# Two output tiles of a weight slab: alternating the single products between their two PSUM banks

## The reference

```python
# first block (cut)
z = rms_norm(x, g_mix) @ w_in
x = x + concat([mla(z...), hgrn2(z...)]) @ w_o
h = rms_norm(x, g_ffn)
x = x + (silu(h @ w_gate) * (h @ w_up)) @ w_down
x = x + sigmoid(rms_norm(x, g_ple) @ w_ple_gate) * (p @ w_ple_proj)
# second block (cut)
q, k, v, g, u, sv, a_ret, a_sgu = split(_rmsnorm(x, g_pre_mix) @ w_in)
merged = sigmoid(a_ret) * retention(q, k, v, g) @ w_ret_o \
       + sigmoid(a_sgu) * spatial_gating(u, sv) @ w_sgu_o
x = x + _rmsnorm(merged @ w_out, g_post_mix)
x = x + _rmsnorm(conv_gated_mlp(_rmsnorm(x, g_pre_ffn)), g_post_ffn)
```

## Time and profile before

| what | value |
|---|---|
| median of three runs | 1727.41 us |
| time of the profiled execution | 1728.11 us |
| its span, first to last instruction | 1726.8 us |
| mean granted clock of TensorE | 0.979 of full speed |
| TensorE matmul busy | 1646.0 us, 95% of the span, 7857 instructions |
| TensorE weight loads busy | 1355.8 us, 7857 instructions |
| VectorE busy | 882.4 us, 51% |
| ScalarE busy | 653.7 us, 38% |
| shares of the chain that ended last | TensorE 91%, VectorE 5%, ScalarE 2% |

### The profile page before, as it was taken

The page is one execution under the profiler, slowest core; times in us unless marked ns, Lnnn a source line. Parts: engine busy times, 40 slices in busy tenths (PEclk is TensorE's granted clock), DMA queues, the critical chain, the costliest instruction groups (busy, mean ns, idle before and its releaser), DMA issues.

```text
span 1726.8 us, 18642 instructions
## 1 busy us (share of the span) xinstructions
PE 1646.0 (95%) x7857; PEld 1355.8 (79%) x7857; DVE 882.4 (51%) x1168; ACT 653.7 (38%) x796; POOL 11.7 (1%) x25
## 2 busy tenths in 40 slices
PE   7999999999999999998999799999997899999997
PEld 6777677778888888776887698888875688888886
DVE  6556556564444422367526533354343777676323
ACT  4546667342222211254423233223232444444211
POOL 1000000000000000000000000000000000000000
PEclk9999999999999999998999999999998899999998
DMA  4321011123333232322321032212222132222221
GB/s 157 92 74 49 25 49 50 49 98 98 98 98 96 97 97 94 112 74 73 104 74 50 25 104 93 95 57 98 98 98 74 49 98 98 98 95 91 97 96 73
DMA packets 120274, 144.28 MB, mean 84 GB/s; under 512 B 6009, under 2 KB 109776, under 8 KB 120192
## 3 DMA queue, kind: packets, MB, share of 16 engines
q1 hardware_dynamic: 118768, 139.87, 24.7%
q0 software_dynamic: 1232, 3.16, 0.6%
q10 hardware_dynamic: 192, 0.07, 0.0%
HBM read 140.99 MB, written 2.10 MB: 83 GB/s over the span
## 4 chain that ended last, share of the span: by engine, by line
PE 91%; DVE 5%; ACT 2%; issue 1%; DMA 1%; SPq 0%; DVEq 0%; ACTq 0%
PE bank L364 27%; PE bank L366 27%; PE bank L365 27%; PE bank L826 1%; PE bank L585 1%; PE bank L584 1%; PE bank L603 1%; PE bank L651 1%; DVE slab_lo L948 1%; PE bank L809 1%; PE bank L632 1%; PE bank L874 1%; PE bank L402 1%; PE bank L646 0%; DVE tmp L961 0%
## 5 line engine op out<-in xcount | busy, mean ns | idle before, releaser
L364 PE MATMUL bank<-h_hi,slab_hi 128*128 128x512 f32 x1320 | 527.3, 399 | 20.5 <-DVE h_lo L953 10.4
L366 PE MATMUL bank<-h_hi,slab_lo 128*128 128x512 f32 x1320 | 519.3, 393 | 0.0
L365 PE MATMUL bank<-h_lo,slab_hi 128*128 128x512 f32 x1320 | 519.3, 393 | 0.0
L948 DVE TENSOR_TENSOR slab_lo<-slab_raw,slab_hi 128x2048 fp32r<-128x2048 f32 x130 | 296.0, 2278 | 326.7 <-ACT slab_hi L1634 326.4
L364 PEld LDWEIGHTS bank<-h_hi,slab_hi 128*128 128x128 f32 x1320 | 251.7, 191 | 81.9 <-issue 27.6
L1634 ACT ACTIVATE slab_hi<-slab_raw 128x2048 fp32r<-128x2048 f32 x130 | 246.3, 1896 | 152.5 <-DMA slab_raw<-in_w_down 142.8
L365 PEld LDWEIGHTS bank<-h_lo,slab_hi 128*128 128x128 f32 x1320 | 251.6, 191 | 53.9 <-issue 2.2
L366 PEld LDWEIGHTS bank<-h_hi,slab_lo 128*128 128x128 f32 x1320 | 251.0, 190 | 53.5
L987 DVE TENSOR_TENSOR tmp<-bank,x_rstd_rows 128x512 f32<-128x512 f32 x98 | 67.2, 687 | 110.7 <-PE bank L366 110.6
L364 PE MATMUL bank<-slab_hi,h_hi 128*128 128x256 f32 x320 | 91.5, 286 | 2.2 <-DVE slab_lo L948 2.2
L366 PE MATMUL bank<-slab_hi,h_lo 128*128 128x256 f32 x320 | 90.5, 283 | 0.0
(11 more groups left out here) (384 smaller groups left out, 1963.9 us busy)
## 6 DMA issues: line engine op xcount, KB each, us to landing
slab_raw<-in_w_in SPq DMA_DIRECT2D x40, 1024.0 KB, 4.9
slab_raw<-in_w_up SPq DMA_DIRECT2D x33, 1024.0 KB, 5.0
slab_raw<-in_w_down SPq DMA_DIRECT2D x22, 1024.0 KB, 4.9
slab_raw<-in_w_gate SPq DMA_DIRECT2D x11, 1024.0 KB, 5.1
slab_raw<-in_w_o SPq DMA_DIRECT2D x4, 1024.0 KB, 4.9
slab_raw<-in_w_ple_gate SPq DMA_DIRECT2D x4, 1024.0 KB, 5.2
slab_raw<-in_w_ret_o SPq DMA_DIRECT2D x4, 1024.0 KB, 4.9
slab_raw<-in_w_sgu_o SPq DMA_DIRECT2D x4, 1024.0 KB, 4.8
```

Source lines behind the costliest of these rows:

```text
L364: T.matmul(ps, a_hi, b_hi, start=start, stop=False, skip_group_check=skip)
L365: T.matmul(ps, a_hi, b_lo, start=False, stop=False, skip_group_check=skip)
L366: return T.matmul(ps, a_lo, b_hi, start=False, stop=stop, skip_group_check=skip)
L948: V.tensor_tensor(w_lo[j][:, 0:n], raw[j][:, 0:n], w_hi[j][:, 0:n].bitcast(F32), ALU.subtract).then_inc(slab_lo, 1)
```

## The change

`slab_fm` no longer calls `three`. For each block k, and for each of the three products, it issues the matmul of tile 0 and then that of tile 1. Every slab, with `ready` or without, now has that order. The number of matmuls, their operands, their banks and the sum of each tile stay the same. Within a tile the order of the products stays the same too. In the 74 slabs without `ready`, the last matmul of tile 0 moves from place 24 of 48 to place 47; that of tile 1 stays at place 48. Two matmuls in a row no longer share the stationary operand or the bank. The waits of a `ready` slab stand where they stood.

```diff
             ps = [take(names[t], 2 * (g % 2) + t) for t in range(2)]
-            for n in range(2 * KT):
-                k, t = (n // 2, n % 2) if ready else (n % KT, n // KT)
-                if ready and t == 0:
+
+            for k in range(KT):
+                if ready:
                     T.wait_ge(ready[k][0], ready[k][1])
-                ins = three(ps[t][:, :], hv[:, k, t * P:(t + 1) * P], lv[:, k, t * P:(t + 1) * P],
-                            src_hi[:, k, :], src_lo[:, k, :], k == 0, k == KT - 1)
-                if k == KT - 1:
-                    whole(names[t], ins)
+                for n, (wv, src) in enumerate(((hv, src_hi), (hv, src_lo), (lv, src_hi))):
+                    for t in range(2):
+                        ins = T.matmul(ps[t][:, :], wv[:, k, t * P:(t + 1) * P], src[:, k, :],
+                                       start=k == 0 and n == 0, stop=k == KT - 1 and n == 2)
+                        if k == KT - 1 and n == 2:
+                            whole(names[t], ins)
```

## The result

| | before | after |
|---|---|---|
| median of five runs | 1727.41 us | 1739.56 us |
| lowest and highest | 1723.20, 1731.61 | 1736.78, 1740.76 |
| time of the profiled execution | 1728.11 us | 1739.56 us |
| its span | 1726.8 us | 1738.3 us |
| mean granted clock | 0.979 | 0.980 |

The difference is 1739.56 - 1727.41 = 12.2 us by the medians and 1738.3 - 1726.8 = 11.5 us by the spans. I had forecast 1744 us, with a range from 1731 to 1760.

What follows compares the result with a forecast made beforehand. TensorE, busy 95% of the span, was taken to bound the kernel. 1728.1 + 11.3 (waits) + 5.1 (clock) = 1744.5 us, less 0.7 for the median of runs: 1743.8, given as 1744 us; range 1731 to 1760 us.

Steps and rivals of the forecast that it cites:

- the pace: Interval between matmuls of `slab_fm`: 226.7 ns each, 10.88 us a slab, forecast to change by 0.
- the clock: Longer waits lower TensorE's clock behind the rotary slabs (2.85 us), first branch (1.14) and second branch (1.1): 5.1 us, between 0 and 6.9.
- the 13 us above: Rival, chance 0.10: no neighbours share weights, so 3936 matmuls of `slab_fm` go to 230 ns, 13 us more, 1757 us.
- the 52 us below: Rival, chance 0.07: alternating banks removes a fixed 13.3 ns from every matmul of `slab_fm`, 52 us less, 1692 us.
- The rule of the Trainium skill: 512-column matmuls cycling through banks make TensorE idle and its clock vary; as a rival, chance 0.02, 89 us, 1833 us.
- The ends of stages: Longer TensorE waits behind embedding gate (2.49 us), rotary slabs (1.70), first branch (1.83) and second branch (2.56): 8.58 us.
- head start: Tile 0's reader starts at L + 0.27, tile 1's at L + 0.5 (L: start of slab's last matmul): 0.23 us.
- The small places: Output projection 0.46 us, three retention gate slabs 1.38, the second slab of all 0.46, and `u` 0.4.
- My bound of twice 0.46: Upper bound for the five places with one more bank read, if ScalarE's squares and silus come in as well.
- In the middle: Mid-stage, tile 0's later work is hidden; up projection's split in time by 0.5 us, `u` late by 0.4 us once.

Runs made afterwards that it cites:

- new order in seventy: Kernel before, with the new order in 70 of 82 slabs, all but the twelve ahead of a place where TensorE waits: 1725.80 us, ratio 0.9997.
- weights changed: Kernel before, tile by tile, products reordered high x high, low x high, high x low so neighbours in these slabs share no stationary operand: 1726.32 us, ratio 0.9998.
- signal alone: Kernel before, matmul order kept; only the signal that tile 0 is whole is raised by the matmul before the slab's last: 1739.36 us, ratio 1.0067.
- new order in twelve: Kernel before, with the new order only in the twelve slabs ahead of a TensorE wait: median 1738.50 us, ratio 1.0077; run again for its trace, 1739.36 us.
- banks one by one, new order: Changed kernel, both down projections wait for each bank ahead of its own first matmul, banks 4 to 7 first in the first slab: 1735.25 us, ratio to before 1.0042.
- banks one by one, old order: Kernel before, tile-by-tile order kept, both down projections wait for each bank ahead of its own first matmul: 1725.43 us, ratio 0.9991.
- three matmuls a tile in turn: Kernel before, all slabs in the order of the ready slabs: per block three matmuls of tile 0, then three of tile 1; 1736.98 us, ratio 1.0051.

## Why the prediction was right, and where its numbers were off

The mechanism held: the pace stays, and the loss lies where TensorE waits for the last two tiles. That 16.4 us of forecast came as near as it did to the 12.2 measured is luck in part. The waits came out at 14.0 us instead of 11.3, and the clock, forecast at 5.1 us more, took less than before in this pair of traces.

**The pace: right.** I took 0 on the word of one `ready` slab. The slab of 10.88 us, the kernel with seventy slabs in the new order (0.9997) and the one with changed weights (0.9998) bear it out. Both bounds are refuted, the 13 us above and the 52 us below: a slab would be 11.04 or 10.2 us. The rule of the Trainium skill that I had weighed (TensorE: Matmul & The Clock Gate, A second HAM failure mode: psum-queue depth-cycling) doesn't show here either: 3936 matmuls in two banks in turn, and a mean clock of 0.980 against 0.979.

**The ends of stages: right, to 0.01 us at four of them.** The work on tile 0 goes in front of that on tile 1 in VectorE's queue, less 0.23 us of head start. The signal moved alone shows that this is the cause. The small places were 0.46, 1.38, 0.46 and 0.4 by forecast and came out at 0.91, 1.1, 0.38 and 0.18. The output projection's was forecast at half of what it is. There ScalarE copies tile 0 and only then squares all eight tiles, and VectorE's chain of seven operations (line 963) waited 0.82 us for these squares, where before it began right behind VectorE's own copy. My bound of twice 0.46 allowed for that.

**In the middle: right.** The up projection has no wait for `slab_lo` in the new trace, and that of `u` is 0.18 us instead of 0.4.

**What I missed: the down projections, 2.85 us.** I wrote that the feed-forward has less work per slab and left its last slab out of the list. That slab's work isn't ahead of a split but ahead of a bank: TensorE takes all eight banks at once. The row of the kernel before, 0.83 us with "issue" beside it, said that something was waited for; 0.83 us is the end of VectorE's read behind the last matmul. The price of one tile's work less the head start was the right rule; the list of places was short. In the changed kernel the read of the last tile stands behind the whole work on the tile before. The timeline of VectorE there:

```profile
601.68 0.69 DVE L1320 TENSOR_TENSOR tmp<-tmp,bank 128x512 f32<-128x512 f32 x1 [4.72 <-PE bank L379]
602.40 0.69 DVE L1322 TENSOR_TENSOR tmp<-tmp,x_rstd_rows 128x512 f32<-128x512 f32 x1
603.79 0.69 DVE L1324 TENSOR_TENSOR hid_lo<-tmp,hid_hi 128x512 fp32r<-128x512 f32 x1 [0.69 <-ACT hid_hi L1920]
604.40 0.68 DVE L1320 TENSOR_TENSOR tmp<-tmp,bank 128x512 f32<-128x512 f32 x1
```

The second read starts 604.40 - 601.68 = 2.72 us after the first and ends at 605.08; TensorE starts at 605.18. Less the head start that is 2.49 us, and 2.48 was measured.

**The term that was mis-sized: the clock, 5.1 us forecast.** I read means over 5.7 us as if the clock stood still in them. Taken over shorter stretches, the view shows it at 0.50 in some and at 1.00 in all others. Behind the embedding gate and behind the second branch, before:

```profile
789.41:796.23 6.82, 5.84 (x14) 0.50 0.25 88
1277.51:1280.93 3.42, 3.42 (x10) 0.50 0.03 9
```

And in the changed kernel, with that behind the rotary slabs in the middle:

```profile
794.05:800.87 6.82, 3.90 (x9) 0.50 0.17 59
862.31:865.73 3.42, 3.42 (x18) 0.50 0.02 7
1285.57:1292.39 6.82, 3.72 (x9) 0.50 0.19 66
```

The second number is the part of the stretch in which TensorE worked, and only that part costs time. Behind the embedding gate the low clock lasted as long as before, but 2.92 us of it fell into the longer wait. That is why the mean behind the wait rose from 0.50 to 0.66. Behind the second branch it lasted twice as long, and 3.10 us of it fell into the wait.

At 0.50 matmuls of 512 columns follow each other at 0.426 us (790.96 to 793.94 us before, seven steps), at 1.00 at 0.227 us. So a low stretch costs 0.47 of the work time in it, which is an estimate for the other kinds of matmuls. The terms, in us:

| behind | low clock under work, before | after | more, at 0.47 | forecast |
|---|---|---|---|---|
| rotary slabs | 0 | 3.42 | 1.6 | 2.85 |
| first branch | 3.41 | 3.41 | 0 | 1.14 |
| second branch | 3.42 | 3.72 | 0.1 | 1.1 |
| embedding gate | 5.84 | 3.90 | -0.9 | 0 |
| first down projection | 0 | 3.42 | 1.6 | 0 |

The forecast places cost 1.7 us and not 5.1. The timeline bears out the first row: from the start behind the rotary slabs to TensorE's next long wait it is 39.50 us (861.20 to 900.70) where it was 38.01 (855.51 to 893.52), 1.5 us more.

At all other places, but for the stretch behind the output projection, the low clock costs about 5.9 us less in the changed kernel's trace than in that of before. I can't credit that to the change: it differs as much between traces of the same kind.

What all traces have in common shows when the clock and the start are taken out of the span. The first slab starts behind the loads of the input, at 24.28 us before and 25.46 us in the changed kernel. The low clock behind the output projection is left out, since TensorE mostly waits for VectorE there: from the first matmul behind that wait to the next wait of this kind (line 402, now 404) it is 27.41 us in both traces. In us:

| kernel | span | first slab at | low clock under work | its cost, at 0.47 | span less start and clock |
|---|---|---|---|---|---|
| before | 1726.8 | 24.28 | 49.7 | 23.3 | 1679.2 |
| new order in seventy | 1726.8 | 24.18 | 49.5 | 23.3 | 1679.3 |
| weights changed | 1724.2 | 24.47 | 43.8 | 20.6 | 1679.2 |
| changed | 1738.3 | 25.46 | 42.3 | 19.9 | 1692.9 |
| signal alone | 1739.9 | 24.80 | 46.8 | 22.0 | 1693.1 |
| new order in twelve | 1738.1 | 24.44 | 44.2 | 20.8 | 1692.9 |
| banks one by one, new order | 1732.0 | 23.88 | 40.3 | 18.9 | 1689.2 |
| banks one by one, old order | 1720.0 | 25.03 | 37.2 | 17.5 | 1677.5 |
| three matmuls a tile in turn | 1737.2 | 24.31 | 53.2 | 25.0 | 1687.9 |

The first three kernels, with the short waits, agree within 0.2 us, the next three, with the long ones, too, and between the two groups lie 13.7 us. The sum of the waits is 13.99. Banks taken one by one make it 3.8 and 1.7 us less, where the waits give 3.6 and 1.3; three matmuls a tile in turn make it 5.1 us less than the changed kernel, where the waits are 4.7 us shorter in sum. So the sum should have been 11.3 + 2.85 - 0.16 (the small places and rounding) = 13.99 us for the waits. The clock should have been a spread about it, not a cost of 5.1 us: from the first row to the fourth it gives 3.4 us back and the start takes 1.2 us, and 13.99 + 1.2 - 3.4 = 11.8 us stands against 11.5 by the spans.

## What to carry to other kernels

When two results that one queue works up in turn are made ready at the same time instead of one behind the other, the matmul engine here lost nothing while it had other work. It lost the work on the first result, less the head start, once at each place where it waited for the second. So list every place where the engine stands still, those marked "issue" and waits for free buffers among them, and price each from the reader's chain; the sum of the waits was good to a few tenths of a microsecond once the list was whole. Don't price the clock by the worst stretch seen: take several traces, and count the low clock under work alone. Whether a suspected order of matmuls costs anything can be told from any stretch of the old trace that has it already.

## What the runs showed of the hardware that I had not expected

Where the clock had already fallen behind a wait of TensorE, a longer wait made that hardly dearer. Behind the embedding gate it stood at 0.50 for 6.82 us after a wait of 3.72 us and after one of 6.21 us, and less of that fell on work after the longer one (3.90 instead of 5.84 us). Behind the first branch it was 3.41 us after 2.48 and after 4.30 us; behind the second, 3.42 us of it fell on work after 3.73 us and 3.72 us after 6.29 us. Behind the rotary slabs there was none after waits of 2.15 to 2.17 us, in four traces, and 3.41 or 3.42 us of it after waits of 3.42 to 3.86 us, in five.

Kernels of one kind differ in it as much as the two kinds do. The time at 0.50 under work, the stretch behind the output projection left out, goes from 37.2 to 49.7 us in the four traces with the short waits, and from 40.3 to 53.2 us in the five with the longer ones. At 0.47 these 12.5 and 12.9 us are some 6 us, half of what the change cost.
